# Latent attention of a one-core transformer kernel: the scores of the first head group made before the second group's query projections

## The chip, the cores and the metric

The kernel runs on one core of a Trainium2 chip. The metric is the device time of one execution in microseconds (us). The engines of the core are TensorE (PE: matrix products and transposes; PEld is its weight load), VectorE (DVE), ScalarE (ACT), GpSimd (POOL), and SyncE (SP), which issues the weight transfers.
## The reference, cut to what matters

The program computes three transformer layers on 256 tokens of width 1024, in nine stages: FFN, RWKV mixer, FFN, FFN, latent attention, FFN, FFN, forgetting attention, FFN. The change touches the fifth stage alone:

```python
def _mla_mixer(h, cos, sin, w_in, q_a_norm, kv_a_norm, w_q_up, w_kv_up, q_norm, k_norm, w_out):
    p = h @ w_in
    c_q, c_kv, k_pe = jnp.split(p, (Q_RANK, Q_RANK + KV_RANK), axis=-1)          # 384, 256, 64
    q = (_rmsnorm(c_q, q_a_norm) @ w_q_up).reshape(B, T, MLA_HEADS, QK_DIM)      # 8 heads of 192
    kv = (_rmsnorm(c_kv, kv_a_norm) @ w_kv_up).reshape(B, T, MLA_HEADS, NOPE_DIM + V_DIM)
    k_nope, v = kv[..., :NOPE_DIM], kv[..., NOPE_DIM:]
    k = concatenate([k_nope, broadcast(k_pe)])
    q, k = _rmsnorm(q, q_norm), _rmsnorm(k, k_norm)       # then rope on the last 64 of q and k
    o = _causal_attention(q, k, v)                        # softmax(q k^T * scale, causal) v
    return o.reshape(B, T, MLA_HEADS * V_DIM) @ w_out
```

## The kernel before

Weights stream from HBM in units of 128 x 3072 float32 (a part "gu" of 2048 columns, a part "dn" of 1024), two buffers for each part. ACT rounds a part to float32r (`hi_gu`, `hi_dn`), DVE or POOL makes the remainder (`lo_gu`, `lo_dn`), and PE forms each product as three matmuls, hi x hi, hi x lo and lo x hi (`three_products`, line 344). SP issues the load of a part when the remainder of the part two units earlier has been made.

The latent attention has eight units. Its eight heads are handled as two groups of four. For each group g PE

- projects the keys, values and queries (the queries of the second group are 36 matmuls of 384 columns, from units 4 and 5),
- transposes them per head in `turn_heads(g)`: 24 transposes (line 1869), 8 for the keys, 8 for the queries, then 4 for the rotated key parts (`krT`) and 4 for the rotated query parts (`qrT`),
- makes the scores in `scores(g)`: per head one mask matmul (line 1939, 384 columns), and true float32 products with 128 rows (line 1941) and with 64 rows (line 1942), of 128 and then of 256 columns. The hardware runs a float32 product as two MATMUL instructions,
- transposes the normalized probabilities and multiplies by the values in `attend(g)` (lines 1971, 1980, 1981), and then projects to the output (`out_row`).

The other engines work between these steps. For the queries ACT copies each head pair out of PSUM and squares it (`queries`, lines 1606 and 1607), DVE sums the squares (`sum_q`, line 1742), ACT makes the inverse root with a logarithm and an exponential (`inverse_roots`, lines 1594 and 1599, each with its own table load), and POOL applies the rotation (`q_rope`, lines 1510 to 1516). `keys_turned` and `rope_turned` (lines 1614, 1619) copy the transposed keys on ACT, `queries_turned` (lines 1758, 1761) the transposed queries on DVE. DVE takes the row maxima of the scores (`shifts`, lines 1768, 1773), ACT the exponentials (`exponentials`, line 1625), DVE the division (`normalized`, lines 1780, 1785).

PSUM has eight banks: group 0 has its queries, transposed heads and scores in banks 0 to 3, group 1 in banks 4 to 7.

The order on each engine is written out by hand, and it is the order of the code. Every step adds one to a counting semaphore of its engine, so that a wait for a step is also a wait for all steps ahead of it in that engine's list (`mla_names`). `turn_heads(1)` waits for the last copy of the queries on ACT, its `krT` and `qrT` transposes for the key copies on ACT and for the rotation on POOL, and `scores(g)` waits for `krT` (ACT) and `qrT` (DVE).

Of the kernel before, what the change touches and what calls it, by code (L numbers as in the profile page):

```python
# [225 lines left out]
def build(nc, units_gu, units_dn, x_in, positions, constants, params, low_rank, final_gain, out, stages=STAGES):  # L226
# [6 lines left out]
    with ExitStack() as ctx:  # L233
# [89 lines left out]
        def lo_gu(dve, pair, p):  # L323
            dve.wait_ge(gu_hi_ready, 2 * pair + p + 1)
            nc.vector.tensor_tensor(gu_lo[:, p, :], raw_gu[:, p, :], gu_hi[:, p, :].bitcast(F32),  # L325
                                    ALU.subtract).then_inc(gu_lo_ready, 1)
# [275 lines left out]
        def unit(s, u):  # L602

            return first_pair[s] + u // 2, u % 2
# [787 lines left out]
        def mla_names():  # L1392
            pe = ["kv_T", ("cq_T", 0), ("cq_T", 1), ("k", 0, 0), ("k", 0, 1), ("v", 0, 0), ("q", 0, 0),
                  ("k", 1, 0), ("v", 1, 0), ("v", 1, 1)]
            turned = lambda g: [(n, g, b) for n in ("kT", "qT") for b in range(2)] + [("krT", g), ("qrT", g)]
            scored = lambda g: [("scores", g, 0), ("scores", g, 1)]
            pe += turned(0) + [("q", 1, 0), ("q", 1, 1)] + scored(0) + turned(1) + scored(1)
            for g in range(2):
                pe += [("probsT", g, 0), ("probsT", g, 1), ("o", g, 0), ("o", g, 1)]
            act = ["sin", "cos", "ss_kv", "c_q", "hi_kv", ("hi_cq", 0), ("hi_cq", 1), "ss_cq",  # L1400
                   ("sq_k", 0, 0), ("sq_k", 0, 1), "ln_kv", "sig_kv", ("v", 0, 0), ("v", 0, 1), ("ln_k", 0), ("rs_k", 0),
                   ("q", 0, 0), ("q", 0, 1), ("sq_k", 1, 0), ("sq_k", 1, 1), ("kT", 0, 0), ("kT", 0, 1),
                   ("v", 1, 0), ("v", 1, 1), ("ln_k", 1), ("rs_k", 1), ("krT", 0), ("ln_q", 0), ("rs_q", 0),
                   ("q", 1, 0), ("q", 1, 1), ("ln_q", 1), ("rs_q", 1), ("exp", 0, 0), ("kT", 1, 0), ("kT", 1, 1),
                   ("krT", 1), ("exp", 0, 1), ("probsT", 0, 0), ("probsT", 0, 1), ("hi", 0, 0), ("hi", 0, 1),
                   ("exp", 1, 0), ("exp", 1, 1), ("probsT", 1, 0), ("probsT", 1, 1), ("hi", 1, 0), ("hi", 1, 1)]
            dve = ["r2", "eps_r2", "inv_r2", "kv", "lo_kv", "is_kv", "rho2", "pe_term", "e_k", ("lo_cq", 0), ("lo_cq", 1),
                   ("ss_k", 0, 0), ("ss_k", 0, 1), "is_q", "e_q", ("k", 0), ("ss_q", 0, 0), ("ss_q", 0, 1),
                   ("ss_k", 1, 0), ("ss_k", 1, 1), ("qT", 0, 0), ("qT", 0, 1), ("qrT", 0), ("k", 1),
                   ("ss_q", 1, 0), ("ss_q", 1, 1)]  # L1410
            score = lambda g, i: [("max", g, i), ("shift", g, i)]
            norm = lambda g, i: [("recip", g, i), ("probs", g, i)]
            dve += score(0, 0) + score(0, 1) + [("qT", 1, 0), ("qT", 1, 1), ("qrT", 1)] + norm(0, 0) + norm(0, 1)
            dve += score(1, 0) + score(1, 1) + [("lo", 0, 0), ("lo", 0, 1)] + norm(1, 0) + norm(1, 1)
            dve += [("lo", 1, 0), ("lo", 1, 1)]
            pool = ["pos", "gain0", "gain", "angle", "turn", "round", "part0", "red0", "part1", "red1", "part2", "red2",
                    "clamp", "minus", "abs", "quarter", "minus_sin", "k_gain", "q_cos", "k_cos", "q_sin", "k_sin",
                    "kpe_cos", "kpe_sin", "kpe_sum", "kpe", ("kr", 0), "mask", ("q_cos", 0), ("q_sin", 0), ("q_rope", 0),
                    ("kr", 1), ("q_cos", 1), ("q_sin", 1), ("q_rope", 1)]
            return {"pe": pe, "act": act, "dve": dve, "pool": pool}  # L1420
# [108 lines left out]
        def mla_act(act, s):  # L1529
# [61 lines left out]
            def inverse_roots(n, g, bias):  # L1591
                wait(act, MS, "dve", (f"ss_{n}", g, 1))
                for t in range(2):
                    ins = nc.scalar.activation(of_heads[f"rs_{n}"][:, g, t, :], of_heads[f"ss_{n}"][:, g, t, :], ACT.Ln,
                                               bias=bias[:, t:t + 1])
                done(ins, (f"ln_{n}", g))
                wait(act, MS, "act", (f"ln_{n}", g))
                both = of_heads[f"rs_{n}"][:, g, :, :]
                done(nc.scalar.activation(both, both, ACT.Exp, scale=-0.5), (f"rs_{n}", g))

            def queries(g, t):
                mla_there(act, s, ("q", g, t))
                wait(act, MS, "dve", ("ss_k", g, t))
                for i in range(2):
                    bank = 4 * g + 2 * t + i
                    cp(qs[:, t, 2 * i:2 * i + 2, :].rearrange("p h c -> p (h c)"), banks[:, bank, 0:2 * QK_DIM])
                    ins = nc.scalar.activation(sq[:, t, i * 2 * QK_DIM:(i + 1) * 2 * QK_DIM], banks[:, bank, 0:2 * QK_DIM],
                                               ACT.Square)
                done(ins, ("q", g, t))
# [11 lines left out]
            def exponentials(g, i):  # L1621
                wait(act, MS, "dve", ("shift", g, i))
                for hh in (2 * i, 2 * i + 1):
                    for b, cols in enumerate(BLOCKS_Q):
                        ins = nc.scalar.activation(probs[g][:, hh, cols], banks[:, 4 * g + hh, cols], ACT.Exp,
                                                   bias=softmax_cols(g, "shift")[:, hh, b:b + 1],
                                                   scale=of_heads["rs_q"][:, g, b, hh:hh + 1],
                                                   accum_out=softmax_cols(g, "sum")[:, hh, b:b + 1])
                done(ins, ("exp", g, i))
# [33 lines left out]
            hi_dn(act, *unit(s, 4))  # L1663
            hi_gu(act, *unit(s, 5))
            inverse_roots("q", 0, MST["e_q"])
            queries(1, 0)
            queries(1, 1)
            inverse_roots("q", 1, MST["e_q"])
            wait(act, MS, "act", ("rs_q", 1))
            exponentials(0, 0)  # L1670
            keys_turned(1)
            rope_turned(1)
            exponentials(0, 1)
            hi_dn(act, *unit(s, 5))
            turned_probs(0, 0)
            turned_probs(0, 1)
# [13 lines left out]
        def mla_dve(dve, s):  # L1690
# [49 lines left out]
            def sum_q(g, t):  # L1740
                wait(dve, MS, "act", ("q", g, t))
                done(nc.vector.reduce_sum(of_heads["ss_q"][:, g, t, :], sq[:, t, :].rearrange("p (h c) -> p h c", h=4), X),
                     ("ss_q", g, t))

            def scaled_k(g):
                wait(dve, MS, "act", ("rs_k", g))
                if g:
                    wait(dve, MS, "pe", ("kT", g - 1, 1))
                for t in range(2):
                    ins = tt(ks[:, t], banks[:, 4 + t, :].rearrange("p (h c) -> p h c", h=4),  # L1750
                             of_heads["rs_k"][:, g, t, :].rearrange("p (h c) -> p h c", c=1).to_broadcast([P, 4, NOPE]),
                             ALU.mult)
                done(ins, ("k", g))
# [23 lines left out]
            def normalized(g, i):  # L1777
                wait(dve, MS, "act", ("exp", g, i))
                heads = slice(2 * i, 2 * i + 2)
                done(nc.vector.reciprocal(softmax_cols(g, "max")[:, heads, :], softmax_cols(g, "sum")[:, heads, :]),  # L1780
                     ("recip", g, i))
                wait(dve, MS, "dve", ("recip", g, i))
                for b, cols in enumerate(BLOCKS_Q):
                    part = probs[g][:, heads, cols]
                    ins = tt(part, part, softmax_cols(g, "max")[:, heads, b:b + 1].to_broadcast(
                        [P, 2, cols.stop - cols.start]), ALU.mult)
                done(ins, ("probs", g, i))
# [19 lines left out]
                sum_k(1, t)  # L1807
            queries_turned(0)
            scaled_k(1)
            lo_gu(dve, *unit(s, 5))  # L1810
            sum_q(1, 0)
            sum_q(1, 1)
            shifts(0, 0)
            shifts(0, 1)
            queries_turned(1)
            normalized(0, 0)
            normalized(0, 1)
            shifts(1, 0)
            shifts(1, 1)
            outputs(0, 0)  # L1820
# [9 lines left out]
        def mla_pe(pe, s):  # L1830
# [113 lines left out]
                    done(ins, ("scores", g, i))  # L1944

            turn_heads(0)
            wait(pe, MS, "dve", ("k", 1))
            wait(pe, MS, "act", ("v", 1, 1))
            for t, i in pairs:
# [7 lines left out]
            for t, i in pairs:  # L1957
                ins = up(banks[:, 4 + 2 * t + i, 0:n], ((4, i * n),), t, w, n, False, True)
                if i:
                    done(ins, ("q", 1, t))  # L1960
            wait(pe, MS, "pool", "mask")
            scores(0)
            turn_heads(1)
            scores(1)

# [414 lines left out]
```

## Time and profile before

| | us |
|---|---|
| three timed runs | 1786.82, 1788.88, 1788.99 (median 1788.88) |
| the profiled execution | 1793.74 |
| its span, first to last instruction | 1792.0 |
| TensorE busy in the span | 1637.2 (91%) |
| VectorE, ScalarE, GpSimd busy | 961.4, 928.6, 95.4 |
| mean granted TensorE clock | 0.947 |

The profiled execution took 4.9 us more than the median. Some 1.7 us of it lie outside the span. The latent attention lies between about 888 and 1003 us of the span. Chains, busy shares and waits say who is late; the granted clock says how long an unchanged PE instruction takes.

### The profile page before, as it was taken

To read this page: it belongs to the slowest core of one execution; us is meant where nothing else is said; L and a number is where in the kernel's file an instruction comes from. 1 tells how busy PE (TensorE), PEld (TensorE's weight loads), DVE (VectorE), ACT (ScalarE), POOL (GpSimd) and SP (SyncE) were. 2 spreads that over 40 slices of the span, in tenths; PEclk is the share of its full clock that TensorE was granted. 3 is DMA by queue.
4 is the path that set the end of the run, shared out by engine and by line. 5 is a ranking of instruction groups with operands and counts; after the bars stand their busy time and mean duration, and the time that the engine had idled before them with its cause. 6 is when DMAs were issued, how large, how long until landed. Compare 5 with 4: busy or idle time off the path is not lost.

```text
span 1792.0 us, 27633 instructions
## 1 busy us (share of the span) xinstructions
PE 1637.2 (91%) x11002; PEld 1495.9 (83%) x11002; DVE 961.4 (54%) x1200; ACT 928.6 (52%) x1164; POOL 95.4 (5%) x88
## 2 busy tenths in 40 slices
PE   5999888688899999999988999999999888689997
PEld 5999788578689998999886899989999775579996
DVE  4555454643355555555554555555554587546554
ACT  5444436322266555655566665556654541556653
POOL 0000003222000002000033000000000000000000
PEclk9999999788899999999999999999999895889998
DMA  5454343100034553554431354444455240125552
GB/s 219 183 196 184 146 151 143 71 1 1 36 129 183 194 185 141 199 184 179 176 141 49 130 209 176 180 172 176 176 189 196 106 176 36 47 80 190 184 191 93
DMA packets 47890, 259.82 MB, mean 145 GB/s; under 512 B 5344, under 2 KB 5600, under 8 KB 26976
## 3 DMA queue, kind: packets, MB, share of 16 engines
q1 hardware_dynamic: 47520, 258.77, 39.1%
q8 instruction: 36, 0.59, 0.1%
q10 hardware_dynamic: 288, 0.34, 0.1%
q14 instruction: 14, 0.11, 0.0%
q0 software_dynamic: 32, 0.00, 0.0%
HBM read 258.04 MB, written 1.05 MB: 145 GB/s over the span
## 4 chain that ended last, share of the span: by engine, by line
PE 81%; DVE 8%; ACT 8%; issue 2%; POOL 0%; DMA 0%; DVEq 0%; ACTq 0%
PE banks L344 70%; ACT gu_hi L316 2%; DVE gu_lo L325 2%; PE banks L1180 1%; PE banks L1186 1%; PE banks L2232 1%; PE banks L2233 1%; ACT h_hi L364 1%; DVE arena L2126 1%; ACT arena L381 1%; DVE x L468 1%; PE banks L1153 1%; PE banks L2234 1%; DVE dn_lo L330 1%; ACT dn_hi L321 1%
## 5 line engine op out<-in xcount | busy, mean ns | idle before, releaser
L344 PE MATMUL banks<-h_hi,gu_hi 128*128 128x256 f32 x2344 | 668.8, 285 | 31.2 <-DVE gu_lo L325 24.0
L344 PE MATMUL banks<-h_lo,gu_hi 128*128 128x256 f32 x2344 | 666.2, 284 | 0.0
L344 PE MATMUL banks<-h_hi,gu_lo 128*128 128x256 f32 x2344 | 666.0, 284 | 0.0
L325 DVE TENSOR_TENSOR gu_lo<-raw_gu,gu_hi 128x2048 fp32r<-128x2048 f32 x162 | 372.2, 2298 | 251.6 <-ACT gu_hi L316 251.2
L344 PEld LDWEIGHTS banks<-h_hi,gu_hi 128*128 128x128 f32 x2344 | 451.5, 193 | 40.6 <-DVE gu_lo L325 22.9
L344 PEld LDWEIGHTS banks<-h_lo,gu_hi 128*128 128x128 f32 x2344 | 451.7, 193 | 4.8 <-issue 0.2
L344 PEld LDWEIGHTS banks<-h_hi,gu_lo 128*128 128x128 f32 x2344 | 451.4, 193 | 0.0
L316 ACT CAST gu_hi<-raw_gu 128x2048 fp32r<-128x2048 f32 x162 | 307.9, 1903 | 48.6 <-PE banks L344 40.6
L483 ACT ACTIVATE silu<-silu 128x256 f32<-128x256 f32 x132 | 55.5, 420 | 342.6 <-DVE silu L491 342.5
L344 PE MATMUL banks<-dn_hi,act_hi 128*128 128x512 f32 x528 | 207.8, 393 | 2.1 <-DVE act_lo L497 2.1
L344 PE MATMUL banks<-dn_lo,act_hi 128*128 128x512 f32 x528 | 207.0, 392 | 0.0
L344 PE MATMUL banks<-dn_hi,act_lo 128*128 128x512 f32 x528 | 205.4, 389 | 0.0
L491 DVE TENSOR_TENSOR silu<-banks,arena 128x256 f32<-128x256 f32 x132 | 56.0, 424 | 257.8 <-PE banks L344 244.6
L330 DVE TENSOR_TENSOR dn_lo<-raw_dn,dn_hi 128x1024 fp32r<-128x1024 f32 (+1 forms) x150 | 179.0, 1194 | 7.5 <-ACT dn_hi L321 7.5
L321 ACT CAST dn_hi<-raw_dn 128x1024 fp32r<-128x1024 f32 (+1 forms) x162 | 166.8, 1032 | 5.9 <-PE banks L344 5.3
L485 ACT CAST act_hi<-act 128x256 fp32r<-128x256 f32 x132 | 53.7, 407 | 131.5 <-DVE act L494 131.5
L344 PEld LDWEIGHTS banks<-dn_hi,act_hi 128*128 128x128 f32 x528 | 99.6, 189 | 22.1 <-issue 4.9
L344 PEld LDWEIGHTS banks<-dn_hi,act_lo 128*128 128x128 f32 x528 | 99.2, 188 | 21.7
L344 PEld LDWEIGHTS banks<-dn_lo,act_hi 128*128 128x128 f32 x528 | 99.6, 189 | 15.7
L497 DVE TENSOR_TENSOR act_lo<-act,act_hi 128x256 fp32r<-128x256 f32 x132 | 56.1, 425 | 62.4 <-ACT act_hi L485 62.4
L344 PE MATMUL banks<-gu_hi,h_hi 128*128 128x512 f32 (+2 forms) x128 | 55.1, 430 | 21.3 <-DVE arena L1750 4.8
L483 ACT ACT_TABLE_LOAD x51 | 65.4, 1283 | 0.9
(319 smaller groups left out, 1671.3 us busy)
## 6 DMA issues: line engine op xcount, KB each, us to landing
raw_gu<-units_gu SPq DMA_DIRECT2D x162, 1024.0 KB, 5.8
raw_dn<-units_dn SPq DMA_DIRECT2D x162, 512.0 KB, 3.3
x<-x_in SPq DMA_DIRECT2D x2, 512.0 KB, 5.0
out<-x SPq DMA_DIRECT2D x1, 1024.0 KB, 3.9
cst<-constants SPq DMA_DIRECT2D x1, 784.0 KB, 12.2
lora<-low_rank SPq DMA_DIRECT2D x1, 512.0 KB, 12.9
arena<-final_gain SPq DMA_DIRECT2D x1, 512.0 KB, 3.9
par<-params ACTq DMA_DIRECT2D x1, 203.0 KB, 6.7
```

Of the source, the lines that this page charges most:

```text
L316: nc.scalar.copy(gu_hi[:, p, :], raw_gu[:, p, :]).then_inc(gu_hi_ready, 1)
L321: nc.scalar.copy(dn_hi[:, p, 0:n], raw_dn[:, p, 0:n]).then_inc(dn_hi_ready, 1)
L325: nc.vector.tensor_tensor(gu_lo[:, p, :], raw_gu[:, p, :], gu_hi[:, p, :].bitcast(F32), ALU.subtract).then_inc(gu_lo_ready, 1)
L330: nc.vector.tensor_tensor(dn_lo[:, p, 0:n], raw_dn[:, p, 0:n], dn_hi[:, p, 0:n].bitcast(F32), ALU.subtract).then_inc(dn_lo_ready, 1)
L344: ins = nc.tensor.matmul(out, a, b, start=first and i == 0, stop=last and i == 2)
L364: ins = nc.scalar.activation(h_hi[:, k, :], banks[:, first_bank(s) + b, i * T:(i + 1) * T], ACT.Copy, scale=pcol("norms", s * KD + k))
L381: nc.scalar.activation(xn[:, t, :], x[:, t, :], ACT.Square, accum_out=sumsq[:, t:t + 1]).then_inc(squares_ready, 1)
L468: nc.vector.scalar_tensor_tensor(out=x[:, t, c * 512:(c + 1) * 512], in0=banks[:, (0 if stages[s] == "mla" else 4) + 2 * t + c, :], scalar ...
L483: nc.scalar.activation(silu[:, p, :], silu[:, p, :], ACT.Silu).then_inc(silu_ready, 1)
L485: nc.scalar.copy(act_hi[:, p, :], act32[:, p, :]).then_inc(act_hi_ready, 1)
L491: nc.vector.tensor_tensor(silu[:, p, :], banks[:, p, 0:T], rstd_row, ALU.mult).then_inc(gate_ready, 1)
L497: nc.vector.tensor_tensor(act_lo[:, p, :], act32[:, p, :], act_hi[:, p, :].bitcast(F32), ALU.subtract).then_inc(act_lo_ready, 1)
```

## The change

On PE `scores(0)` now follows `turn_heads(0)` directly, ahead of the 36 matmuls of the second group's queries; before it stood behind them. ACT makes both exponentials of group 0 ahead of the second group's query copies, where they stood behind `inverse_roots("q", 1)`, one of them also behind the key copies of group 1. DVE takes the maxima of group 0 ahead of the remainder of unit 5, then normalizes group 0, and only then sums the squares of the second group's queries and copies their transposes. POOL and SP keep their order. No instruction is added or removed.

```diff
@@ mla_names @@
-            pe += turned(0) + [("q", 1, 0), ("q", 1, 1)] + scored(0) + turned(1) + scored(1)
+            pe += turned(0) + scored(0) + [("q", 1, 0), ("q", 1, 1)] + turned(1) + scored(1)
...
-                   ("q", 1, 0), ("q", 1, 1), ("ln_q", 1), ("rs_q", 1), ("exp", 0, 0), ("kT", 1, 0), ("kT", 1, 1),
...
+                   ("exp", 0, 0), ("exp", 0, 1), ("q", 1, 0), ("q", 1, 1), ("ln_q", 1), ("rs_q", 1), ("kT", 1, 0), ("kT", 1, 1),
@@ mla_act @@
             inverse_roots("q", 0, MST["e_q"])
+            wait(act, MS, "act", ("rs_q", 0))
+            exponentials(0, 0)
+            exponentials(0, 1)
             queries(1, 0)
             queries(1, 1)
             inverse_roots("q", 1, MST["e_q"])
             wait(act, MS, "act", ("rs_q", 1))
-            exponentials(0, 0)
             keys_turned(1)
             rope_turned(1)
-            exponentials(0, 1)
             hi_dn(act, *unit(s, 5))
@@ mla_dve @@
             scaled_k(1)
+            shifts(0, 0)
+            shifts(0, 1)
             lo_gu(dve, *unit(s, 5))
+            normalized(0, 0)
+            normalized(0, 1)
             sum_q(1, 0)
             sum_q(1, 1)
-            shifts(0, 0)
-            shifts(0, 1)
             queries_turned(1)
-            normalized(0, 0)
-            normalized(0, 1)
             shifts(1, 0)
@@ mla_pe @@
             turn_heads(0)
+            wait(pe, MS, "pool", "mask")
+            scores(0)
             wait(pe, MS, "dve", ("k", 1))
             wait(pe, MS, "act", ("v", 1, 1))
...
-            wait(pe, MS, "pool", "mask")
-            scores(0)
             turn_heads(1)
             scores(1)
```

The order of PE in the latent attention before, from the 24 transposes of `turn_heads(0)` to the first head's scores; the 36 projection matmuls of line 344 stand between them (three of them are shown, `gu_hi`, `gu_lo` are the parts of the weights, `h_hi`, `h_lo` those of the activations):

```order
1821 L1869 MATMUL banks<-cst,arena 128x128 x24
1822 L344 MATMUL banks<-gu_hi,h_hi 128x384
...
1856 L344 MATMUL banks<-gu_lo,h_hi 128x384
1857 L344 MATMUL banks<-gu_hi,h_lo 128x384
1858 L1939 MATMUL banks<-act_hi,act_lo 128x384
1859 L1941 MATMUL banks<-arena 128x128
```

The same place on PE in the changed kernel, with the first and last rows of the scores and of the projections:

```order
1821 L1869 MATMUL banks<-cst,arena 128x128 x24
1822 L1939 MATMUL banks<-act_hi,act_lo 128x384
1823 L1941 MATMUL banks<-arena 128x128
...
1841 L1942 MATMUL banks<-arena 128x256
1842 L344 MATMUL banks<-gu_hi,h_hi 128x384
...
1877 L344 MATMUL banks<-gu_hi,h_lo 128x384
1878 L1869 MATMUL banks<-cst,arena 128x128 x24
```

The scores moved ahead of the projections, so that the projections now stand directly in front of the transposes of `turn_heads(1)`.

The order of ACT before, from the last copy of the second group's queries to the copies of its transposed keys (`krT` is the row of line 1619):

```order
266 L1607 ACTIVATE arena<-banks 128x384
267 L1594 ACT_TABLE_LOAD
268 L1594 ACTIVATE mla_stats<-mla_stats 128x4 x2
269 L1599 ACT_TABLE_LOAD
270 L1599 ACTIVATE mla_stats<-mla_stats 128x8
271 L1625 ACTIVATE arena,small<-banks,small,mla_stats 128x128
...
275 L1614 COPY arena<-banks 128x512 x2
276 L1619 COPY arena<-banks 128x512
```

The same place on ACT in the changed kernel (the lines above 1400 are one lower there), from the last exponential of group 0:

```order
266 L1624 ACTIVATE arena,small<-banks,small,mla_stats 128x256
267 L1605 COPY arena<-banks 128x384
...
274 L1606 ACTIVATE arena<-banks 128x384
275 L1593 ACT_TABLE_LOAD
276 L1593 ACTIVATE mla_stats<-mla_stats 128x4 x2
277 L1598 ACT_TABLE_LOAD
278 L1598 ACTIVATE mla_stats<-mla_stats 128x8
279 L1613 COPY arena<-banks 128x512 x2
280 L1618 COPY arena<-banks 128x512
```

The eight copies and squares, the inverse root and the key copies now stand behind each other, with the exponentials ahead of them all.

## Rows read from the trace of the kernel before

**Rows 1.** The chain that ended last, shares of the span by engine (the page):

```profile
PE 81%; DVE 8%; ACT 8%; issue 2%; POOL 0%; DMA 0%; DVEq 0%; ACTq 0%
```

**Rows 2.** PE in the stage: start, duration, engine, line, operation [idle before <-releaser]:

```profile
936.35 2.78 PE L1869 MATMUL banks<-cst,arena 128*128 128x128 f32 x24
943.93 0.69 PE L344 MATMUL banks<-gu_hi,h_hi 128*128 128x384 f32 x1 [4.79 <-DVE arena L1750]
...
953.13 0.34 PE L1939 MATMUL banks<-act_hi,act_lo 128*128 128x384 f32 x1
...
953.62 0.48 PE L1942 MATMUL banks<-arena 64*128 64x128 f32 x2
954.04 0.70 PE L1941 MATMUL banks<-arena 128*128 128x256 f32 x2
954.66 0.70 PE L1942 MATMUL banks<-arena 64*128 64x256 f32 x2
955.29 0.44 PE L1939 MATMUL banks<-act_hi,act_lo 128*128 128x384 f32 x1
...
962.09 2.84 PE L1869 MATMUL banks<-cst,arena 128*128 128x128 f32 x24
965.81 0.41 PE L1939 MATMUL banks<-act_hi,act_lo 128*128 128x384 f32 x1 [0.88 <-DVE small L1780]
...
974.85 1.53 PE L1971 MATMUL banks<-cst,arena 128*128 128x128 f32 x12
```

**Rows 3.** Stretches: us, PE busy (instructions), PEclk, DMA share, GB/s:

```profile
939.30:943.80 4.50, 0.00 (x0) 0.94 0.00 0
943.90:950.00 6.10, 6.07 (x19) 0.50 0.33 95
950.20:953.10 2.90, 2.90 (x18) 1.00 0.84 329
953.10:962.10 9.00, 9.00 (x39) 1.00 0.01 4
...
965.80:974.80 9.00, 8.99 (x36) 1.00 0.16 58
...
1477.40:1517.00 39.60, 39.60 (x96) 0.50 0.11 40
1526.99:1530.40 3.41, 3.38 (x16) 0.50 0.00 0
```

**Rows 4.** PE in the scores of the forgetting attention:

```profile
1487.38 0.79 PE L2232 MATMUL banks<-arena 64*128 64x128 f32 x2
1488.11 0.79 PE L2233 MATMUL banks<-cst,arena 8*128 8x128 f32 x2
...
1489.25 1.22 PE L2232 MATMUL banks<-arena 64*128 64x256 f32 x2
1490.40 1.22 PE L2233 MATMUL banks<-cst,arena 8*128 8x256 f32 x2
```

**Rows 5.** ACT in the latent attention:

```profile
942.46 0.57 ACT L1619 COPY arena<-banks 128x512 f32<-128x512 f32 x1
...
952.29 0.48 ACT L1606 COPY arena<-banks 128x384 f32<-128x384 f32 x1 [3.20 <-PE banks L344]
...
954.89 0.57 ACT L1607 ACTIVATE arena<-banks 128x384 f32<-128x384 f32 x1
...
958.58 0.21 ACT L1599 ACTIVATE mla_stats<-mla_stats 128x8 f32<-128x8 f32 x1
...
962.79 1.08 ACT L1614 COPY arena<-banks 128x512 f32<-128x512 f32 x2 [0.89 <-PE banks L1869]
```

**Rows 6.** DVE in the latent attention:

```profile
945.80 2.83 DVE L325 TENSOR_TENSOR gu_lo<-raw_gu,gu_hi 128x2048 fp32r<-128x2048 f32 x1 [1.93 <-ACT gu_hi L316]
...
957.66 1.02 DVE L1768 TENSOR_REDUCE small<-banks 128x2 f32<-128x256 f32 x2 [1.21 <-PE banks L1942]
```

**Rows 7.** POOL, the end of the second group's query rotation:

```profile
958.44 1.26 POOL L1516 TENSOR_TENSOR arena<-arena 128x512 f32<-128x512 f32 x1
```

More of the change, by code:

```diff
@@ L1403, in mla_names @@
                    ("v", 1, 0), ("v", 1, 1), ("ln_k", 1), ("rs_k", 1), ("krT", 0), ("ln_q", 0), ("rs_q", 0),
-                   ("q", 1, 0), ("q", 1, 1), ("ln_q", 1), ("rs_q", 1), ("exp", 0, 0), ("kT", 1, 0), ("kT", 1, 1),
-                   ("krT", 1), ("exp", 0, 1), ("probsT", 0, 0), ("probsT", 0, 1), ("hi", 0, 0), ("hi", 0, 1),
+                   ("exp", 0, 0), ("exp", 0, 1), ("q", 1, 0), ("q", 1, 1), ("ln_q", 1), ("rs_q", 1), ("kT", 1, 0), ("kT", 1, 1),
+                   ("krT", 1), ("probsT", 0, 0), ("probsT", 0, 1), ("hi", 0, 0), ("hi", 0, 1),
                    ("exp", 1, 0), ("exp", 1, 1), ("probsT", 1, 0), ("probsT", 1, 1), ("hi", 1, 0), ("hi", 1, 1)]
@@ L1408, in mla_names @@
                    ("ss_k", 0, 0), ("ss_k", 0, 1), "is_q", "e_q", ("k", 0), ("ss_q", 0, 0), ("ss_q", 0, 1),
-                   ("ss_k", 1, 0), ("ss_k", 1, 1), ("qT", 0, 0), ("qT", 0, 1), ("qrT", 0), ("k", 1),
-                   ("ss_q", 1, 0), ("ss_q", 1, 1)]
+                   ("ss_k", 1, 0), ("ss_k", 1, 1), ("qT", 0, 0), ("qT", 0, 1), ("qrT", 0), ("k", 1)]
             score = lambda g, i: [("max", g, i), ("shift", g, i)]
             norm = lambda g, i: [("recip", g, i), ("probs", g, i)]
-            dve += score(0, 0) + score(0, 1) + [("qT", 1, 0), ("qT", 1, 1), ("qrT", 1)] + norm(0, 0) + norm(0, 1)
-            dve += score(1, 0) + score(1, 1) + [("lo", 0, 0), ("lo", 0, 1)] + norm(1, 0) + norm(1, 1)
+            dve += score(0, 0) + score(0, 1) + norm(0, 0) + norm(0, 1) + [("ss_q", 1, 0), ("ss_q", 1, 1)]
+            dve += [("qT", 1, 0), ("qT", 1, 1), ("qrT", 1)] + score(1, 0) + score(1, 1) + [("lo", 0, 0), ("lo", 0, 1)] + norm(1, 0) + norm(1, 1)
             dve += [("lo", 1, 0), ("lo", 1, 1)]
```

## The prediction

> **What bounds the kernel now.** I read the chain that ended last first. PE holds 81% of it [rows 1], so a microsecond of PE that is lost in the latent attention is lost at the end. Next I read PE's timeline of that stage [rows 2]: the 24 transposes of the first group end at 939.13 (936.35 + 2.78), PE idles 4.79 us for the scaled keys of the second group, the 36 query matmuls run from 943.93 to 953.13 (9.20), the first scores to 962.09 (8.96), the second transposes 2.84, an idle 0.88, and the second scores from 965.81 to 974.85 (9.04). Third I read the granted clock [rows 3]. It falls in the idle stretch. The first 19 projection matmuls take 6.10 us at 0.50 (1.2 GHz), 0.32 each; afterwards 18 take 2.90 at 1.00 (2.4 GHz), about 0.17 with those that lap over the edge. At full clock the 36 would take 36 x 0.173 = 6.24, so the fall costs 9.20 - 6.24 = 2.96. Both score blocks run at 1.00 throughout. The last view is the one place where scores of another stage start after an idle stretch: the forgetting attention computes them for 39.6 us without a break, and the clock is 0.50 in all of it [rows 3].
>
> **Part 1, the start of the first scores.** They wait for the copy `krT` on ACT. ACT keeps its order up to there, so it ends at 942.46 + 0.57 = 943.03 [rows 5], and the scores start at 943.07 where the projections started at 943.93: -0.86. PE still idles 3.9 of the 4.8 us. The mask and `qrT` are there long before.
>
> **Part 2, at what clock the first scores run.** Before, the idle stretch was paid by projection matmuls, which pack PE densely and had the clock back after 6.1 us. Now it is paid by scores. A score matmul leaves gaps: the 256-column pair takes 0.63 (954.66 to 955.29) and the 128-column pair of 64 rows 0.42 (953.62 to 954.04) even at full clock [rows 2], far from the pace of line 344. The same kinds of instructions in the forgetting attention (64 rows, and some of 8) take 0.73 and 1.15 a pair (1487.38 to 1488.11, 1489.25 to 1490.40) [rows 4], 1.74 and 1.83 times as long, and never got the clock back. So the likeliest is that the first scores stay at 1.2 GHz to their end. A bound from above for their length is twice the 8.96, 17.9; from below 1.74 x 8.96 = 15.6 if it stays low. I take 16.0, nearest to the two measured ratios: +7.0. If the clock comes back as it did for the projections, the loss is about 3.0 instead; that is a rival, and it stays in the range. No gain is possible here, since 1.00 is the highest clock.
>
> The Trainium skill (TensorE: Matmul & The Clock Gate, section "Part 1: The HAM clock gate") says that the throttle is released after a short sustained burst of activity, and its "What you observe" shows plain back-to-back matmuls getting there in some microseconds. By that rule the first scores would lose about 3 us, not 7. The 39.6 us at 0.50 with PE shown busy all the time [rows 3] speak against reading "busy" off the busy column, so I let the trace decide and keep the rule as the first rival.
>
> **Part 3, the query projections.** They start at low clock, as before, and being dense they bring it back, as before: 9.20, no change. Their length could lie between 6.24 (full clock at once) and 36 x 0.32 = 11.5. The remainder of unit 5 that their last third needs is now made behind `shifts(0, 1)`. That is 1.02 and a small operation after the scores (about 1.3), and then at most 2.83 [rows 6]: 4.1 after the scores' end. PE needs it after 24 matmuls, which is 24 x 0.32 = 7.7 later (4.2 at full clock). It is hidden; without the cover it would cost up to 0.1. SP's next load (unit 7, its trigger is this remainder) starts some 14 us later than before, still 20 us ahead of its use. The exponentials (2.1 us each) lie beside the projections, and ACT is free when the first queries are ready. ACT's new self-wait costs nothing, since the value was there long before.
>
> **Part 4, the gap ahead of the second scores.** Call the end of the projections Q. `turn_heads(1)` waits for ACT's last query copy. Before, the scores of the first group covered the copies, sums, roots and rotation. Now nothing does. From the rows of before, with Q = 953.13: the copies end at 954.89 + 0.57 = 955.46, so Q + 2.33; the inverse root is made at 958.58 + 0.21 = 958.79, Q + 5.66; POOL's rotation ends at 959.70, Q + 6.57 [rows 5, 7]. The two key copies on ACT stand behind the root and take 1.08: Q + 6.75. Only then may PE transpose `qrT` (4 of 24 transposes, 2.84 x 4/24 = 0.47 at full clock, 0.9 at half), and DVE copies it in 0.7. The second scores start at Q + 8.2 at full clock, at Q + 8.8 if it has fallen. Before, all but the score block between Q and 965.81 was 12.68 - 8.96 = 3.72. So the part costs +4.5 to +5.1; I take 5.1. DVE does its sums in time: its division of the first group ends before the copies do.
>
> **Part 5, the second scores.** In these 8.8 us PE works only on 24 transposes, in three pieces. The 4.5 us without PE work made the clock fall before [rows 3]; here the idle parts are 2.3 and about 2 and 1 us with transposes between them. I think that the clock falls: then the second scores run at 1.2 GHz too, +7.0 (between 0 and +9.0, twice 9.04). Afterwards the 12 transposes of `attend(0)` (1.53 at full clock [rows 2]) and the 2.9 us of value products run slower until the clock is back. That is +1.1 to +3.6; the transposes of the forgetting attention were 3.41 us at 0.50 before it rose [rows 3], so I take +2.0. The same page of the Trainium skill, section "Part 4: PE-mode transpose", says that a transpose does not count as work for the clock in the way a matmul does. By that the fall in the gap is nearly certain and the tail is +3.6; no row settles it, since in the forgetting attention the clock rose behind transposes.
>
> **The sum.** -0.86 + 7.0 + 0 + 5.1 + 7.0 + 2.0 = +20.2 us against the profiled execution. The moments at which the clock falls and rises differ from execution to execution: a fall that comes a microsecond into a score block saves 0.45, and projections that have the clock back earlier than after 6.1 us save up to 1. For these I subtract 1.1: +19.1. The profiled execution took 1793.74, the median of the runs is 1788.88; the sum is made of differences, so I put it on the median: 1788.9 + 19.1 = 1808.0.
>
> **The rivals.** First, the clock comes back inside the scores, in both blocks, after about the time that the projections took: -0.86 + 3.0 (first scores) - 3.0 (the projections now begin at full clock) + 4.8 + 2.8 = +6.7, 1795.6. For it speaks that the scores of this stage hold 1.00 once they have it [rows 3], and that half of their products have 128 rows. Against it speak the 39.6 us. Second, the first block is low but the clock survives the second gap, because of its transposes: -0.86 + 7.0 + 0 + 4.5 = +10.6, 1799.5. Against it speaks how little PE does there. Third, the one on the other side: the idle stretch of 3.9 us is short enough that the clock stays up, and the second gap doesn't take it either. Then the 2.96 us of the projections are won back, and only the gap is left: -0.86 - 2.96 + 4.5 = +0.7, 1789.6, not slower. It decides if PEclk at the first scores is 1.00. Against it speaks that the 0.94 of the 4.5 idle us [rows 3] puts the fall near their end, which is for it as well: the fall came after about 4 us of idle time in this execution. If in addition part of the gap were covered, it would be faster; nothing in the rows shows such a cover. That the change doesn't do what it says can be left out: the order of PE is what moved.
>
> **The numbers.** The forecast (both blocks low) has 0.62, the first rival 0.13, the second 0.13, the third 0.12. This kernel's runs differ by about 0.12%, so 0.2%, 3.6 us, is what can be told from no change. The third rival is mostly within it: 0.09 same, 0.03 faster; the others are slower, 0.88. The forecast's own range is 1802 to 1812.5 (block lengths of 15.6 to 17.9). The range that leaves out the third rival and a little above is 1793.5 to 1812.5.
>
> **What would show it.** In the profile of the changed kernel: PE's idle time ahead of the first score matmul is 3.9 us; PEclk is 0.50 from there to the first projections; the first block takes 16 us, the projections 9, the gap 8.8 with the idle parts released by ACT (query copies, key copies) and DVE; the second block takes 16 at 0.50. I am wrong if PEclk rises within a score block, or if it is 1.00 at the start of one.

## The result: 1.3% slower, and the profile after

| | before | after |
|---|---|---|
| timed runs, median | 1788.93 (4) | 1814.01 (1812.21 to 1814.88, 4) |
| ratio | | 1.0134, 95% interval 1.0121 to 1.0147 |
| profiled execution; its span | 1793.74; 1792.0 | 1814.88; 1813.1 |

The time rose by 25.1 us where I forecast 19.1; 1814.0 is 1.5 us above my range. PE in the stage after (columns as in [rows 2], which it answers):

```profile
943.74 0.46 PE L1939 MATMUL banks<-act_hi,act_lo 128*128 128x384 f32 x1 [3.99 <-ACT arena L1618]
...
946.43 1.22 PE L1942 MATMUL banks<-arena 64*128 64x256 f32 x2
947.58 0.69 PE L1939 MATMUL banks<-act_hi,act_lo 128*128 128x384 f32 x1
...
951.65 0.69 PE L1939 MATMUL banks<-act_hi,act_lo 128*128 128x384 f32 x1
...
959.78 0.69 PE L344 MATMUL banks<-gu_hi,h_hi 128*128 128x384 f32 x1
...
970.66 3.14 PE L1869 MATMUL banks<-cst,arena 128*128 128x128 f32 x16 [2.22 <-ACT arena L1606]
974.70 1.94 PE L1869 MATMUL banks<-cst,arena 128*128 128x128 f32 x8 [0.89 <-ACT arena L1613]
977.51 0.66 PE L1939 MATMUL banks<-act_hi,act_lo 128*128 128x384 f32 x1 [0.87 <-DVE arena L1761]
...
993.75 2.82 PE L1971 MATMUL banks<-cst,arena 128*128 128x128 f32 x12
...
1001.63 0.50 PE L344 MATMUL banks<-gu_hi,h_hi 128*128 128x512 f32 x1 [1.40 <-DVE h_lo L1792]
```

And the granted clock in its pieces, the first idle stretch, the first scores, the projections in two parts, the second scores and the work behind them (answers to [rows 3]):

```profile
939.80:943.70 3.90, 0.00 (x0) 1.00 0.00 0
944.00:959.70 15.70, 15.70 (x36) 0.50 0.10 34
959.80:964.40 4.60, 4.60 (x15) 0.50 0.00 0
964.50:968.40 3.90, 3.90 (x23) 1.00 0.64 256
977.60:993.70 16.10, 16.10 (x36) 0.50 0.10 33
993.80:998.50 4.70, 4.70 (x20) 0.50 0.01 2
```

Both score blocks run at 1.2 GHz, the first after its first 0.3 us, the second from end to end. One head takes 4.07 us (947.58 to 951.65) where it took 2.26, a quarter of the 9.04 of a block. PE is shown busy without a break, so neither the busy share nor a wait tells of it; only PEclk does, and the longer instructions. The change added no more than some 3 us of waits (the 2.22, 0.89 and 0.87 in place of 0.88 [rows 2]).

### The profile page after: what moved, and what is told of

The parts are those of the page before. It is cut to its first block, busy times and chain, and to the rows that moved or that the text cites. A ratio compares the mean times of both kernels' runs of the same rounds, so it can differ in the third digit from the quotient of the medians.

```text
span 1813.1 us, 27634 instructions
## 1 busy us (share of the span) xinstructions
PE 1655.0 (91%) x11002; PEld 1506.2 (83%) x11002; DVE 960.6 (53%) x1200; ACT 928.7 (51%) x1164; POOL 93.3 (5%) x88
## 4 chain that ended last, share of the span: by engine, by line
PE 80%; ACT 8%; DVE 8%; issue 2%; POOL 0%; DMA 0%; DVEq 0%; ACTq 0%
PE banks L344 68%; ACT gu_hi L316 2%; DVE gu_lo L325 2%; PE banks L1180 1%; PE banks L1186 1%; ACT h_hi L364 1%; PE banks L2232 1%; PE banks L1942 1%; PE banks L2233 1%; PE banks L1941 1%; DVE arena L2126 1%; DVE dn_lo L330 1%; ACT arena L381 1%; DVE x L468 1%; PE banks L1153 1%
```

## The experiments

**The changed kernel again.** Unchanged, three rounds.

> The changed kernel once more, with a second profile. My theory: the granted clock is 0.50 in the whole of both score blocks, so they take 16.3 us each, and the stage is 20 us longer than before. If so the profile repeats 0.50 there, and the time is 1812 to 1815. Rival: the low clock in the score blocks was a matter of where the execution happened to start; then this profile shows 1.00 in a part of one block and 2 to 7 us less in the span.

Median 1812.85, ratio 1.0106 (1.0082 to 1.0129). The second profile repeats the first, span 1812.5. The two blocks:

```profile
943.30:958.90 15.60, 15.60 (x36) 0.50 0.11 35
...
977.00:993.00 16.00, 16.00 (x36) 0.50 0.10 33
```

One of the four executions took 1803.93 at a mean clock of 0.939 (the others 1811.9 to 1814.3 at 0.933 to 0.935). So the low clock in both blocks is the rule. The 10 us of the one execution are about what one block at full clock and the work behind it would save (7.2 and 1.8 us below); it left no profile, so that a block was spared is read from its time alone.

**Fills.** The next three put dense matmuls whose results nobody reads into the idle stretches. In the kernel before, 20 of them:

```diff
+            def warm(n, bank, p):
+                for _ in range(n):
+                    mm(banks[:, bank, :], h_hi[:, 0, 0:P], gu_hi[:, p, 0:512], start=True, stop=True)
             turn_heads(0)
+            wait(pe, MS, "act", ("v", 1, 1))
+            warm(20, 6, 0)
             wait(pe, MS, "dve", ("k", 1))
```

> The kernel before, with 20 dense matmuls of 512 columns (results unused) put into the 4.8 us in which PE idles ahead of the second group's query projections. My theory: the clock stays at 1.00, the projections take 6.7 us instead of 9.2 (they have to wait some tenths for the remainders of units 4 and 5, made at 946.5 and 948.6), and the time falls by 2.0 to 2.9 us, 0.11 to 0.16%. Rival: the low clock is not caused by the idle stretch; then the projections stay at 9.2 us and the time is the same or 0.3 us worse.

1789.29 against 1790.57, ratio 0.9996 (0.9987 to 1.0005). In the profile the projections run at 1.00 and take 7.0 us (942.17 to 949.15), near the 6.7 expected:

```profile
942.30:949.15 6.85, 6.59 (x37) 1.00 0.41 108
```

So the idle stretch is what takes the clock from them. In the time the expected 2.0 to 2.9 us did not come; the gain is below what can be told. The second profile of before, below, suggests why: there the projections lose 1.5 us, not the 3 of my trace.

In the changed kernel the same with `warm(16, 6, 0)` ahead of `scores(0)`:

> The changed kernel with 16 such dense matmuls in the 3.9 us of idle PE ahead of the first scores. My theory: the first block runs at 1.00 (9.0 us, -7.3), the projections at 1.00 (6.3, about -1.5), the second gap and the second block stay as they are: -9 us against the changed kernel, about 1805. If the clock survives the second gap now, the second block takes 9.0 as well and the time is about 1796. Rival (a score block is slow there for another reason than the clock, e.g. its operands or banks): no change.

1792.74, ratio 1.0023 (1.0007 to 1.0040), 20.1 us below the changed kernel in the same rounds (1812.85): more than the 9 that I gave the first block and the projections, and more than the 17 with the second block. The clock in the first scores, the projections, the transposes, the last part of the gap and the second scores:

```profile
941.30:950.30 9.00, 9.00 (x37) 1.00 0.19 60
950.40:956.60 6.20, 6.20 (x37) 1.00 0.22 69
959.00:962.20 3.20, 3.12 (x15) 0.50 0.00 0
962.40:965.10 2.70, 1.30 (x10) 1.00 0.00 0
965.10:974.10 9.00, 8.99 (x36) 1.00 0.19 60
```

The same operands, banks and order take 9.0 us, so it was the clock. In the unfilled second gap it fell and came back, during transposes, before the scores. Nothing fills that gap, so this half of the gain is luck, but luck of which the times show much: eight of ten executions took 1790.3 to 1794.2, two took 1802.2 and 1804.2, about 10 us more, as much as a score block at 1.2 GHz with what follows costs (no profile of such an execution was taken). The profiles show one difference. Here the clock falls while PE still idles, before the transposes start at 959.08, and it is back after them; in both profiles of the unfilled kernel it falls when they have been running for about 0.6 us, and stays low. That this decides it was not tried.

With both gaps filled (16 ahead of `scores(0)` again, then 9 ahead of `turn_heads(1)`, 8 ahead of its `krT`, 3 ahead of `scores(1)`):

> The changed kernel with the first gap filled and 9, 8 and 3 dense matmuls in the three idle pieces between the projections and the second scores. My theory: both blocks at 1.00, and only the uncovered chain of ACT copies, root, key copies and rotation is left of the change: -0.9 (earlier start) - 3.0 (projections) + 4.5 (gap), +0.6 against before, up to +2 if the dense matmuls overshoot the gaps: 1789 to 1791. Rival (the order itself costs more, by waits on ACT or DVE): above 1793.

1793.19, ratio 1.0013 (1.0003 to 1.0022), and all ten executions lie between 1792.3 and 1793.8. Both blocks:

```profile
941.20:950.20 9.00, 9.00 (x38) 1.00 0.19 60
...
965.20:974.20 9.00, 8.98 (x36) 1.00 0.18 60
```

The long executions are gone, and +2.3 us by the ratio is left. I had 0.6, up to 2, and the time is above the 1793 that I had given to the rival (the order costs by waits). Most of the miss is no wait, though: my 0.6 took off 3.0 us for the projections, and the second profile of before has 1.5 to give; with that the same sum is +2.1. Nor is +2.3 the whole cost of the order, since the kernel before still pays for its projections. Against the kernel before with its own gap filled, from the first transposes to the output projection, it is 45.7 us (934.64 to 980.30) in place of 42.35 (934.57 to 976.92): +3.3. That is the uncovered chain of the second gap (8.4 us in place of 3.7), less the earlier start (0.8) and shorter projections (6.4 in place of 7.0).

**Only the second gap filled.**

> The changed kernel with dense matmuls only in the three idle pieces of the second gap, the first gap left idle. My theory: the first block stays at 0.50 (16.3 us), the projections bring the clock back (8 to 9.5 us), the fill keeps it, the second block takes 9.0: about 1803 (+12 against before, the same place as the one execution of 1803.9 among those of the changed kernel). Rival: the second block is at 0.50 whatever stands ahead of it, because the first was: 1813.

1802.68, ratio 1.0075 (1.0058 to 1.0092). The 1803 expected. First scores, then the filled gap and the second scores:

```profile
942.00:957.40 15.40, 15.40 (x36) 0.51 0.11 35
...
966.10:974.50 8.40, 7.94 (x46) 1.00 0.00 0
974.60:983.60 9.00, 9.00 (x37) 1.00 0.17 60
```

The low first block costs 9.1 us in the stage against both filled (54.8 from the first transposes to the output projection in place of 45.7), 6.8 of them in the block itself and most of the rest in the projections behind it. The second block is at 1.00 although the first was low: it follows the gap ahead of it, not the first block.

**What in the scores keeps the clock down.** The changed kernel without the products of 64 rows in the first block (the rotated parts of four heads are left out):

```diff
...
-                            ins = mm(banks[:, h, cols], qrT[...], krT[...], start=False, stop=q == 1)
+                            if g == 1:
+                                ins = mm(banks[:, h, cols], qrT[...], krT[...], start=False, stop=q == 1)
```

> The changed kernel without the products of 64 rows (the rotated parts) in the first score block; per head the mask and the float32 products of 128 rows are left. If it is the 64-row products and the gaps at them that keep the clock down, the clock returns to 1.00 inside the block or right at its end: the block, about 2.2 us a head at 0.50, shows 1.00 in its last part. If float32 products as such keep it down, the whole block is at 0.50. The profile decides; the time falls anyway by about 8 us, because there is less work.

The one execution took 1788.88. The clock falls 0.4 us into the block, which lasts from 941.23 to 946.08, and is back after 3.4 us, still inside it:

```profile
941.30:942.30 1.00, 1.00 (x6) 0.67 0.00 0
942.30:944.90 2.60, 2.60 (x10) 0.50 0.02 6
945.00:946.00 1.00, 1.00 (x7) 0.97 0.36 57
```

So float32 products of 128 rows bring it back like the projections do; with 64-row products between them, 16 us don't. Whether it is their rows or the gaps at them was not tried. The second block, which keeps its 64-row products, runs at 1.00 here too, with no fill ahead of it: as with the first gap filled, the clock fell in the second gap just before the transposes and was back before the scores:

```profile
955.30:958.60 3.30, 3.15 (x15) 0.50 0.00 0
958.80:961.40 2.60, 1.30 (x10) 1.00 0.00 0
```

That, and not the missing products alone, is why the time fell by some 24 us where I had expected 8.

**The kernel before again.** Unchanged, for a second profile.

> The kernel before, a second profile. The profiled execution of before took 1793.7, above nearly all of its other runs. If it was a chance draw of the clock's falls, this profile has a span some 2 to 5 us shorter with the same order of waits, and the difference lies in stretches at 0.50 of a different length (the projections of the latent attention among them, up to 1.5 us). If the profile always costs that much, the span is 1792 again.

One execution, 1789.05, span 1787.3. The idle stretch and the projections:

```profile
937.30:942.00 4.70, 0.00 (x0) 0.96 0.00 0
942.10:945.10 3.00, 3.00 (x10) 0.50 0.00 0
945.20:949.80 4.60, 4.60 (x28) 1.00 0.74 233
```

The projections take 7.75 us (942.05 to 949.80) where my trace had 9.20 [rows 2]. From the first transposes to the output projection this execution needs 43.1 us, my trace 44.6, and the other 3.2 us of the two spans lie outside the stage, in the clock again: the matmuls at 445 to 452 us, for one, run at 0.52 in my trace and at 1.00 here. Of the 59 timed runs of before, those of the result and of the experiments, the median is 1789.9, and two reach 1793.7. I had forecast from a rare execution.

**The same fill where scores run longest.** The kernel before, with 28 dense matmuls ahead of the scores of the forgetting attention:

```diff
             wait(pe, FX, "act", ("evac", 15))
+            for _ in range(28):
+                mm(banks[:, 2, :], h_hi[:, 0, 0:P], h_hi[:, 0:2, :].rearrange("p k t -> p (k t)"), start=True, stop=True)
             wait(pe, FX, "dve", "neg")
```

> The kernel before, with 28 dense matmuls in the 6.6 us of idle PE ahead of the scores of the forgetting attention, which run 39.6 us at 0.50. If the idle stretch is what takes the clock and scores merely don't bring it back, these scores (products of 64 and of 8 rows) now run at 1.00 and take about 22 us: -17 us, 1773. If products of so few rows can't even hold the clock, it falls a few us into the block and the gain is 1 to 3 us: 1788. No gain at all would say that the idle stretch has no part in it.

1786.81 against 1789.69, ratio 0.9982 (0.9972 to 0.9991): 0.2% faster than the kernel before, the smaller of the two gains that I had set out. The projections of the latent attention take 7.81 us in this profile, which makes two profiles near 7.8 and one, mine, at 9.2. The fill, then the scores:

```profile
1467.80:1473.60 5.80, 5.80 (x26) 1.00 0.26 106
1473.80:1478.20 4.40, 4.40 (x20) 1.00 0.00 0
1478.30:1509.90 31.60, 31.60 (x76) 0.50 0.15 50
```

These scores start at 2.4 GHz and don't hold it: it falls some 4.5 us in, with PE shown busy all the time. The block takes 36.4 us in place of 40.1. The scores of 128 and 64 rows hold 1.00 for 9 us [rows 3]; those of 64 and 8 rows don't. It is a fall without any idle stretch.

**Both fills in the kernel before** (20 and 25 matmuls).

> The kernel before with both fills: 20 dense matmuls ahead of the second group's query projections and 25 ahead of the scores of the forgetting attention. The two gains were 1.3 us (inside its interval) and 2.9 us alone. If they add, as they should when each only keeps the clock in its own stage: about 4 us below before, ratio 0.9975 to 0.998. If the first is no gain in plain executions, the ratio is that of the second alone, 0.998 to 0.9985.

1787.90 against 1790.74, ratio 0.9984 (0.9975 to 0.9993). 4 us were expected if they add, and 2.8 came, as from the second fill alone (2.9); the interval leaves both open. In this profile the scores of the forgetting attention lose the clock after 2.0 us.

**The second gap's chain.** The changed kernel, all gaps filled (4 matmuls in place of 8 ahead of the second group's `krT`), with `keys_turned(1)` and `rope_turned(1)` ahead of `inverse_roots("q", 1)` on ACT.

> The changed kernel with all gaps filled, and on ACT the key copies and the copy of krT ahead of the second group's inverse root (4 dense matmuls in place of 8 in the second piece). If the second gap is the serial chain that I read (query copies, root, key copies, then qrT), it is now ended by the rotation on POOL, and the second scores start about 7.9 us after the end of the projections in place of 8.5. If another wait holds it, the 8.5 stay.

The last wait ahead of `qrT` changes hands, and the scores start 8.2 us after the projections (958.76 to 966.93) where the filled kernel needs 8.4 (956.81 to 965.22):

```profile
965.40 0.66 PE L1869 MATMUL banks<-cst,arena 128*128 128x128 f32 x4 [0.91 <-POOL arena L1515]
```

So POOL's rotation now ends the wait, as the chain had it, but only 0.2 us came of the expected 0.6. The profile of the changed kernel shows that little more was to be had: there the rotation ends at 974.86 (973.59 + 1.27), the key copies at 975.04 (973.97 + 1.07). This is one execution; its time, 1793.97, says nothing of 0.2 us.

## Why the direction was right and the size was not

- **Start of the first scores:** -0.86 forecast. The idle stretch shrank by 0.80 (4.79 to 3.99). Right.
- **First scores at 1.2 GHz:** +7.0 forecast; 16.04 (943.74 to 959.78) in place of 8.96, +7.1. Right, and shown by the fill.
- **Projections:** 0 forecast, bring the clock back. They do; 8.5 (959.78 to Q = 968.3) in place of 9.2, -0.7. Hidden remainder of unit 5: no wait for it. Right.
- **Second gap:** +5.1 forecast from Q to the second scores. Measured 9.2 (968.3 to 977.51) in place of 3.7, +5.5: query copies, root and key copies, as read, with the rotation 0.2 us ahead of them.
- **Second scores:** +7.0 forecast, 16.24 (977.51 to 993.75) in place of 9.04, +7.2. Right; in one execution of eight the time suggests that they, or the first, were spared.
- **Behind them:** +2.0 forecast, 7.9 (993.75 to 1001.63) in place of 6.05 (974.85 to 980.90), +1.8. The row of before:

```profile
980.90 0.50 PE L344 MATMUL banks<-gu_hi,h_hi 128*128 128x512 f32 x1 [1.40 <-DVE h_lo L1792]
```

Trace against trace this is +20.1, where the sum said +20.2. **The step that failed is the last one**, the way from the sum to the time: "I subtract 1.1" and "I put it on the median". I took the other moments of falling and rising as a saving of the changed kernel. Its two profiles show no such saving: the blocks are low from the first tenths on. The kernel before is the one that saves: its projections lose 1.5 us, not 3.0, in the second profile. And my trace of before lay 4.9 us above its own median, which a sum of differences does not cure when the terms (9.20 for the projections) are read from that rare execution; the changed kernel's profiled execution lies 0.9 above its own.

The miss of 6.0 is made of these: 1.1 subtracted, 3.9 because the one execution lies 4.8 above its median and the other 0.9, and 1.1 by which the two traces differ outside the stage (1814.88 - 1793.74 = 21.1 against 20.1 in it), less the 0.1 of the sum. That the terms of the stage add up to within 0.1 is in part luck: the 0.7 that the projections saved makes up for the 0.4 of the gap and the 0.3 of the two blocks.

Against the second profile of before the stage costs 64.7 - 43.1 = 21.6, and by the pooled medians (1813.8 of eight runs, 1789.9 of 59) the change is +23.9. The 2.3 us between the two lie outside the stage, where both kernels are the same program. The profiles show where a part of them goes: the matmuls at 445 to 452 us run at 0.54 and 0.51 in the two profiles of the changed kernel, as at 0.52 in my trace of before, and at 1.00 in its second one. Why that falls more often on the changed kernel stays open. The range failed for the same reason: its upper end allowed for longer blocks, not for the 4.9 us.

The first rival (the clock returns within the scores) is refuted by both traces, the third (it never falls) by the 0.50. The second (first block low, second not) is what the kernel with the second gap filled does; the times of 1803.9, and of 1802.2 and 1804.2 with the first gap filled, fit it or its mirror image, without a profile. The rule of the Trainium skill (TensorE: Matmul & The Clock Gate, "Part 1: The HAM clock gate") that sustained activity releases the throttle agrees with the traces for the projections (the clock is back after 3.0 to 6.2 us) and not for these scores, if activity means PE shown busy: they are, for 15.7 and 16.1 us. Its "Part 4: PE-mode transpose", by which transposes in that mode don't count in the same way, does not fit the transposes of this kernel: the clock rose during them at about 962.3 with the first gap filled, when PE had done nothing else since it fell. Whether they run in the mode that the page means, no trace here shows.

## What to carry to other kernels

After a stretch of PE that takes the clock (here 4.0 us with nothing in it, or 9.2 us with 24 transposes), the work that stands first pays for it: dense matmuls of 128 rows had the clock back in 3 to 6 us, the scores with 64-row products did not get it back in 16, though they hold it for their 9 us once they have it; those of 64 and 8 rows didn't even hold it. So put the dense work behind the wait and the sparse work behind the dense work, and before moving sparse work ahead read PEclk of every stretch that starts after a gap. When a forecast is made from one profiled execution that lies well above the median of the runs, find the terms that differ from execution to execution and widen the range by that distance.

## What the runs showed that I had not expected

- The clock can fall with PE shown 100% busy: the scores of 64 and 8 rows lose 2.4 GHz after 4.5 us in one profile and after 2.0 in another.
- It can rise during transposes in a half-idle stretch (959.0 to 962.2 at 0.50, from 962.4 at 1.00).
- Sixteen useless matmuls, 3.9 us of PE time in an idle stretch, are worth 20 us here: some 10 for the block behind them, and the rest because the second block then mostly has the clock too.
